# Two gate tiles join the seven-product quads, and the first two tiles of the attention mix are cut by heads and by high and low parts

## The chip, the cores and the metric

The kernel runs on one core of a Trainium2 chip. TensorE multiplies, VectorE (DVE), ScalarE (ACT) and GpSimd (POOL) work on the results, and SyncE (SP) and GpSimd start transfers between device memory and the on-chip buffer. The metric is the device time of one launch in microseconds (us). Three runs of the kernel before took 1771.04 to 1771.19 us, with a median of 1771.18.

## What is computed

One layer of a decoder over 1024 tokens of width 1024. The part that the change touches is the merge of three mixers:

```
z  = xn @ W_in            # q | k | v | conv B | conv C | conv h | pool u | 3 branch gates of 1024
gates  = sigmoid(z[gates] + b_gate)
merged = gates[A] * (y_attn @ w_attn_proj)      # the attention mix: y_attn is 1024 tokens x 8 heads of 128
       + gates[B] * (y_conv @ w_conv_proj)
       + gates[C] * (y_pool @ w_pool_proj)      # y_pool = (trailing means of u - u), times small matrices
x = x + rms_norm(merged @ w_out);  x = x + rms_norm(SwiGLU(rms_norm(x)))
```

## The kernel before

**Precision.** Every fp32 operand is held as a high part (`HH`) and a low part (`LL`), and a product is three passes (`PASSES`): high by high, high by low, low by high. A matmul is 128x128 weights against 512 tokens. A plain tile of 128 output columns over 1024 tokens is thus 2 halves x 8 blocks x 3 passes = 48 matmuls (`job`, or `half_job` for one half).

**Quads.** Most of `W_in` from the convolution's columns on is worked in pairs of tiles by seven products of 12 matmuls in place of eight (`x_quad` on each engine; the list is `XQ`, 16 quads long). The sums of inputs that this needs are held in `s_op1` to `s_op4`. A quad's seventh product, `x_third` (weights `B22`, operand `s_op4`), is put into the next quad, since it goes into a bank that the others must have left. The quads use two sets of three of the eight PSUM banks in turn. Each quadrant of a result is combined by DVE, put through the sigmoid by ACT in `stage`, and stored to device memory by POOL (the stores in its `x_quad` loop, semaphores `stage_stored`).

**The end of the quads.** The last two gate tiles (2048+768 to 2048+1023 of the gates) are plain tiles: the first half of one, then the last quad's `x_third`, then the other three halves. After them comes the attention mix: eight tiles of `w_attn_proj`, whose moving operand `ya` (high and low part of eight heads) lies where `s_op1` to `s_op4` lay. POOL's `load_ya` brings `ya` in four transfers of 2 MB, each when the products that read the `s_op` under it are done; the last of them, the low part of heads 4 to 7, waits for `x_third`. TensorE waits for all four before the mix.

**What follows on the other engines.** POOL stores the two plain gate tiles, loads gates (`load_gate`, three buffers, two of them over `stage` and one over the raw sums) and loads the pooling input `u` into `u_pad` (four transfers of 512 KB), which lies over `xn`. DVE goes through the mix tiles in a fixed order (the loop over `m`): it makes the low part of the next weight tile, works out the pooling difference `d_raw` from `u_pad` (`pool_d(m)`, for m below 4), and only then multiplies the mix tile `m` out of PSUM by its gate into `merged`. The four banks 0 to 3 go round: mix tile m+2 (or a small pooling product put between) may start when the tile before in its banks is taken out. The weight ring has two slots, so tile m+2's weights are split after tile m is done. SP loads weights in the order in which they are split (`load`). All order is written out by hand and held by semaphores.

Of the kernel before, what the change touches and what calls it, by code (L numbers as in the profile page):

```python
# [72 lines left out]
def build(nc, x, g_pre_mix, w_in, b_gate, lambda_q1, lambda_k1, lambda_q2, lambda_k2, subln_g,  # L73
# [21 lines left out]
    G_TAIL = 2 * TT + 8  # L95
    G_ATTN = G_TAIL + 4
    G_CONV = G_ATTN + 2 * KT + 2 * 4
# [5 lines left out]
    with ctx:  # L103
# [144 lines left out]
        def proj_bank(first, part):  # L248
# [74 lines left out]
                     ("B12", 0): (first_landed[6], 32), ("B12", 1): (first_landed[7], 48),  # L323
                     ("B22", 0): (first_landed[7], 48), ("B12", 2): (x_pair_landed[0], 160),
                     ("B22", 1): (x_pair_landed[0], 160), ("B22", 2): (x_pair_landed[1], 144)}
        d_landed = [sem(f"d_landed{i}") for i in range(6)]
# [6 lines left out]
        out_stored = x_first[1]  # L333
        x1_landed = tail_stored[0]


# [25 lines left out]
        for j in (0, 2):  # L362
            XQ += [("U", OFF_POOL + j * P, j * P), ("G", OFF_GATE + D + j * P, D + j * P)]
        XQ += [("G", OFF_GATE + D + j * P, D + j * P) for j in (4, 6, 8, 10, 12)]
        NQ = len(XQ)
        X_QUAD_BANKS = (BANKS[1], BANKS[0])

# [97 lines left out]
        def _(sp):  # L465
# [49 lines left out]
            sp.wait_ge(x_products, made(NQ - 1, "P1"))  # L515
            for j in range(6, 8):
                load(tile_of(w_in, OFF_GATE + 2 * D + P * j))
            for m in range(KT):
# [111 lines left out]
        def _(pool):  # L630
# [142 lines left out]
            def load_ya(part, half, products):  # L773


                pool.wait_ge(x_products, products)
                h = slice(4 * half, 4 * half + 4)
                pool.dma_start(ya[:, part, h, :].bitcast(F32),
                               y_dram[h].rearrange("h p (s t) -> p s h t", s=2)[:, part]).then_inc(y_landed, 16)

# [40 lines left out]
            load_gate(0)  # L821
            for j in range(2):
                for half in range(2):
                    gi = G_TAIL + 2 * j + half
                    pool.wait_ge(evacuated[gi % 4], gi // 4 + 1)
                pool.dma_start(gate_dram[2 * D + P * (6 + j):2 * D + P * (7 + j), :], stage[:, j, :])\
                    .then_inc(tail_stored[j], 16)
            pool.wait_ge(tail_stored[0], 16)
            load_gate(1)

            pool.wait_ge(groups_done, G_ATTN)
            for b in range(4):
                pool.wait_ge(stage_stored[b], 16 * quads_of("GU", NQ))
            for c in range(4):
                pool.dma_start(u_pad[:, c, 16:16 + S], u_dram[P * c:P * (c + 1), :]).then_inc(u_landed, 16)
            for buf in (u_pad[:, :, 0:16], sum_a[:, 0:16], sum_b[:, 0:16]):
                pool.memset(buf, 0.0).then_inc(pads_ready, 1)
            pool.wait_ge(tail_stored[1], 16)
            load_gate(2)
            for n in range(3, 18):  # L840
# [116 lines left out]
        def _(act):  # L957
# [336 lines left out]
            direct_part(NQ - 1)  # L1294
            for j in range(2):
                if j:
                    split_next()
                for b in (2 * j, 2 * j + 1):
                    act.wait_ge(stage_stored[b], 16 * quads_of("GU", NQ))
                sigmoid(lambda half: part_of(stage, j, half), bias_g[:, 2 * KT + 6 + j:2 * KT + 7 + j])  # L1300

# [7 lines left out]
            for m in range(KT):  # L1309
                split_next()  # L1310
                if m == 0:
                    split(w_pool[:, HH].rearrange("p g c -> p (g c)"), elems=512, free=(groups_done, g.at()))
                if m < 4:
                    act.wait_ge(d_ready, 2 * m + 2)
                    copy(yp[:, HH, m, :], d_raw[:, :]).then_inc(d_hi, 1)
                else:
                    split(yc[:, HH, m - 4, :], free=(d_lo, 4))
                g.next(2)
                if 2 <= m < 6:
                    pool_out(m - 2)  # L1320
# [225 lines left out]
        def _(dve):  # L1546
# [353 lines left out]

            for j in range(2):
                split_next()
                g.next(2)

# [38 lines left out]
            for m in range(KT):  # L1943
                split_next()
                if m == 0:
                    split(lambda s: w_pool[:, s].rearrange("p g c -> p (g c)"), elems=512)
                if m < 4:
                    pool_d(m)
                else:
                    split(lambda s: yc[:, s, m - 4, :])  # L1950
# [335 lines left out]
            for g in range(4, STEPS):  # L2286
# [15 lines left out]
                if g >= 5 * FC + 5 and g % 2 == 0 and (g - 5 * FC - 5) // 2 < 4:  # L2302
                    if g == 5 * FC + 5:
                        dve.wait_ge(g3_landed, 16)
                        dve.wait_ge(x1_landed, 16 * (TT + 1))
                    finish((g - 5 * FC - 5) // 2)
# [12 lines left out]
        def _(pe):  # L2319
# [263 lines left out]
            pe.wait_ge(xs_lo, 1)  # L2583
            for j in range(2):
                wait_evacuated(pe, g, j - 4)
            for q in range(NQ):
                x_quad(q)
            half_job(xn, 0)
            x_third(NQ - 1)
            half_job(xn, 1)  # L2590
            job(xn)

# [4 lines left out]

            pe.wait_ge(y_landed, 16 * 4)
            for m in range(KT):
                job(ya)  # L2600
                if m == 1 or m >= 5:

                    n.next()
# [181 lines left out]
```

## Time and profile before

| what | value |
|---|---|
| median of three runs | 1771.18 us |
| the profiled execution | 1771.71 us, its span 1769.8 us |
| TensorE busy | 1758.9 us, 99% of the span, 8497 matmuls |
| DVE, ACT, POOL busy | 65%, 42%, 14% |
| granted TensorE clock | 0.999 on average |
| DMA | 213.68 MB, 121 GB/s on average |

Times in the rows are microseconds from the first instruction of the span. A row of the timeline merges equal instructions that follow each other: its start, how long they took together, engine, line, operation, what is written from what is read, and the count. A bracket at the end gives the idle time of that engine before the row and who ended it. TensorE's ends are modelled, so the step from one row's start to the next is the better measure than the length that it gives. The line numbers are those of the helpers for most matmuls and for all splits.

### The profile page before, as it was taken

How to read it: one execution, taken by the hardware profiler on the slowest of the kernel's cores; microseconds unless marked ns; L12 is line 12 of the kernel's file. 1: busy time of each engine (PE TensorE's matmuls, PEld its weight loads, DVE VectorE, ACT ScalarE, POOL GpSimd, SP SyncE). 2: the span in 40 equal slices, each digit the busy share in tenths (PEclk: the TensorE clock that was granted, in tenths of full speed). 3: DMA queues.
4: the chain of work that ended last, by engine and by line, in shares of the span. 5: the costliest groups of instructions: out<-in, count | busy, mean ns of one | idle time of the engine just before them, and what ended most of it. 6: DMA issues, size and time to landing. Idle time of an engine off the chain costs nothing.

```text
span 1769.8 us, 25045 instructions
## 1 busy us (share of the span) xinstructions
PE 1758.9 (99%) x8497; PEld 1455.0 (82%) x8497; DVE 1151.7 (65%) x1863; ACT 739.1 (42%) x1486; POOL 250.7 (14%) x557
## 2 busy tenths in 40 slices
PE   9999999999999999999999999999999999999998
PEld 7887888888888888888888888888888888888886
DVE  5328989999885774443465655776665655567676
ACT  5316666666743323443231123343333333344553
POOL 3221222222120001111100102101010000000011
PEclk9999999999999999999999999999999999999999
DMA  7421222222142222326735712223232322673443
GB/s 242 144 84 49 72 73 71 72 71 71 51 145 87 88 65 99 128 101 230 251 108 168 247 60 95 96 95 126 106 107 102 117 89 94 232 280 98 147 142 125
DMA packets 138041, 213.68 MB, mean 121 GB/s; under 512 B 7569, under 2 KB 94097, under 8 KB 136930
## 3 DMA queue, kind: packets, MB, share of 16 engines
q1 hardware_dynamic: 109200, 108.54, 19.4%
q0 software_dynamic: 28752, 104.04, 16.2%
q8 instruction: 46, 0.75, 0.2%
q14 instruction: 41, 0.34, 0.1%
q10 hardware_dynamic: 2, 0.00, 0.0%
HBM read 150.17 MB, written 62.39 MB: 120 GB/s over the span
## 4 chain that ended last, share of the span: by engine, by line
PE 98%; DVE 1%; issue 0%; ACT 0%; DMA 0%; POOL 0%; DVEq 0%; POOLq 0%; ACTq 0%
PE ps L2340 26%; PE ps L2672 22%; PE ps L2540 17%; PE ps L2728 12%; PE ps L2424 11%; PE ps L2440 4%; PE ps L2348 3%; PE ps L2462 2%; PE ps L2464 1%; DMA x_tile<-in_x_dram 0%; DVE pt L1559 0%; DVE ring L1559 0%; DVE neg_max L1672 0%; DVE ps L1669 0%; ACT e_t L1084 0%
## 5 line engine op out<-in xcount | busy, mean ns | idle before, releaser
L2728 PE MATMUL ps<-d_op 128*128 128x512 f32 x924 | 210.3, 389 | 0.1
L2728 PEld LDWEIGHTS ps<-d_op 128*128 128x128 f32 x924 | 173.3, 188 | 36.9 <-DVE d_op L1559 0.5
L2672 PE MATMUL ps<-s_op,t_op_T 128*128 128x512 f32 x720 | 169.9, 389 | 0.0
L2424 PE MATMUL ps<-xn,ring 128*128 128x512 f32 x672 | 167.1, 398 | 0.0
L2672 PEld LDWEIGHTS ps<-s_op,t_op_T 128*128 128x128 f32 x720 | 135.2, 188 | 28.0
L2424 PEld LDWEIGHTS ps<-xn,ring 128*128 128x128 f32 x672 | 122.5, 188 | 24.8 <-issue 0.2
L2540 PE MATMUL ps<-s_op,x_op_T 128*128 128x512 f32 x576 | 135.9, 389 | 0.0
L2540 PEld LDWEIGHTS ps<-s_op,x_op_T 128*128 128x128 f32 x576 | 108.1, 188 | 22.4
L2672 PE MATMUL ps<-hn,t_op_B 128*128 128x512 f32 x480 | 115.1, 389 | 0.0
L2672 PEld LDWEIGHTS ps<-hn,t_op_B 128*128 128x128 f32 x480 | 90.1, 188 | 18.7
L1084 ACT ACTIVATE e_t<-ps,neg_max 128x256 f32<-128x256 f32 (+7 forms) x128 | 94.1, 740 | 16.5 <-DVE neg_max L1672 15.1
L1559 DVE TENSOR_TENSOR t_op_B<-pair,t_op_B 128x512 fp32r<-128x512 f32 x60 | 41.4, 689 | 90.8 <-ACT t_op_B L963 90.8
L963 ACT ACTIVATE d_op<-rf_pieces 128x512 fp32r<-128x512 f32 x87 | 53.8, 629 | 106.6 <-PE ps L2728 101.1
L1559 DVE TENSOR_TENSOR d_op<-rf_pieces,d_op 128x512 fp32r<-128x512 f32 x87 | 59.3, 691 | 59.9 <-ACT d_op L963 59.9
L1672 DVE TENSOR_REDUCE neg_max<-ps 128x1 f32<-128x256 f32 (+7 forms) x128 | 91.0, 752 | 2.2
L2540 PE MATMUL ps<-xn,x_op_B 128*128 128x512 f32 x384 | 92.1, 389 | 0.0
L2340 PE MATMUL ps<-w_v,xn 128*128 128x512 f32 x384 | 90.5, 395 | 0.0
L2340 PE MATMUL ps<-w_o,ring 128*128 128x512 f32 x384 | 89.0, 391 | 0.0
L2340 PE MATMUL ps<-ya,ring 128*128 128x512 f32 x384 | 87.8, 389 | 0.0
L2340 PEld LDWEIGHTS ps<-w_v,xn 128*128 128x128 f32 x384 | 72.4, 190 | 15.1 <-DVE xn L1559 0.3
L2540 PEld LDWEIGHTS ps<-xn,x_op_B 128*128 128x128 f32 x384 | 72.1, 188 | 14.9
L2340 PEld LDWEIGHTS ps<-ya,ring 128*128 128x128 f32 x384 | 72.1, 188 | 14.9
(270 smaller groups left out, 3374.7 us busy)
## 6 DMA issues: line engine op xcount, KB each, us to landing
pair<-in_w_gate_up_dram SPq DMA_DIRECT2D x20, 1024.0 KB, 5.2
rf_pieces<-s_scratch SPq DMA_DIRECT2D x74, 256.0 KB, 2.7
x_pair<-in_w_in_dram SPq DMA_DIRECT2D x16, 1024.0 KB, 6.2
raw<-in_w_in_dram SPq DMA_DIRECT2D x26, 512.0 KB, 4.0
s_scratch<-gated_ff POOLq DMA_DIRECT2D x40, 256.0 KB, 2.5
gate_in<-gate_scratch POOLq DMA_DIRECT2D x18, 512.0 KB, 3.8
v_scratch<-v_out POOLq DMA_DIRECT2D x32, 256.0 KB, 2.6
vh<-v_scratch POOLq DMA_DIRECT2D x16, 512.0 KB, 5.3
```

Of the source, the lines that this page charges most:

```text
L963: return act.activation(dst, src, ACT.Copy, **kw)
L1084: act.activation(e_t[:, i % 2, c, 0:w], ps[:, 2 * c:2 * c + 2, :].rearrange("p a b -> p (a b)")[:, 0:w], ACT.Exp, bias=neg_max[:, i % 2, c ...
L1559: return dve.tensor_tensor(dst, src, hi.bitcast(F32), ALU.subtract)
L1672: dve.tensor_reduce(neg_max[:, i % 2, c:c + 1], ps[:, 2 * c:2 * c + 2, :].rearrange("p a b -> p (a b)")[:, 0:P * (i + 1)], AX_X, ALU.max, ...
L2340: last = pe.matmul(ps[:, bank, :], lhs, rhs, start=i == 0, stop=i == len(pairs) - 1)
L2348: last = pe.transpose(ps[:, TB[b], P * k:P * (k + 1)], src[:, P * k:P * (k + 1)], ident[:, :])
L2424: last = pe.matmul(ps[:, proj_bank(first, half), :], proj_weights(which, par, a)[:, P * k:P * (k + 1)], xn[:, b, k, HALF * half:HALF * (ha ...
L2440: last = pe.matmul(ps[:, 2 * c + chunk, 0:w], qt[rows, par, a, P * i:P * (i + 1)], kt[rows, par, b, HALF * chunk:HALF * chunk + w], start= ...
L2462: pe.matmul(ps[:, U_BANK, 0:2 * HV], pt[:, i % 2, HH, k, :], vh[:, par, :, k, :], start=k == 0, stop=k == i, skip_group_check=True)
L2540: last = pe.matmul(ps[:, bank, :], x_op[name][:, a, k, :], block(b, k), start=opens and (k, a, b) == (0, HH, HH), stop=(k, a, b) == (3, LL ...
L2672: last = pe.matmul(ps[:, bank, :], t_op[name][:, a, k, :], block(b, k), start=opens and (k, a, b) == (0, HH, HH), stop=(k, a, b) == (3, LL ...
L2728: last = pe.matmul(ps[:, DOWN_BANKS[product][i], :], d_op[:, g % 4, a, P * i:P * (i + 1)], d_op[:, g % 4, 2 + b, :], start=opens and (a, b ...
```

## The change

The two plain gate tiles become a 17th quad in `XQ`. The set of banks that a quad starts with is turned round, so that the last quad again uses banks 4 to 6 and leaves banks 0 to 3 to the mix. The mix's tiles 0 and 1 are worked by `mix_part`: the passes that read the high part of `ya` (two of three) for heads 0 to 3 of tile 0, then the last quad's `x_third`, then the high passes of heads 4 to 7, then those of tile 1, and at the end the passes that read the low part, of tile 0 and then of tile 1. Each of the four transfers of `ya` has its own semaphore, and TensorE waits for each where it is first read. POOL no longer stores the plain tiles and no longer waits for their products; it waits until the last quad's quadrants are stored, loads gates 1 and 2, and then `u`.

```diff
-    G_ATTN = G_TAIL + 4
+    G_ATTN = G_TAIL
...
+        ya_landed = {(HH, 0): (y_landed, 16), (HH, 1): (tail_stored[1], 16), (LL, 0): (early_stored[0], 16 * 5),
+                     (LL, 1): (early_stored[1], 16 * 3)}
...
-        XQ += [("G", OFF_GATE + D + j * P, D + j * P) for j in (4, 6, 8, 10, 12)]
+        XQ += [("G", OFF_GATE + D + j * P, D + j * P) for j in (4, 6, 8, 10, 12, 14)]
         NQ = len(XQ)
-        X_QUAD_BANKS = (BANKS[1], BANKS[0])
+        X_QUAD_BANKS = BANKS
...
             sp.wait_ge(x_products, made(NQ - 1, "P1"))
-            for j in range(6, 8):
-                load(tile_of(w_in, OFF_GATE + 2 * D + P * j))
...
             pool.wait_ge(xt_lo, 7 * NQ)
             load_gate(0)
-            for j in range(2):
-                for half in range(2):
-                    gi = G_TAIL + 2 * j + half
-                    pool.wait_ge(evacuated[gi % 4], gi // 4 + 1)
-                pool.dma_start(gate_dram[2 * D + P * (6 + j):2 * D + P * (7 + j), :], stage[:, j, :])\
-                    .then_inc(tail_stored[j], 16)
-            pool.wait_ge(tail_stored[0], 16)
-            load_gate(1)
-
-            pool.wait_ge(groups_done, G_ATTN)
             for b in range(4):
                 pool.wait_ge(stage_stored[b], 16 * quads_of("GU", NQ))
+            for n in (1, 2):
+                load_gate(n)
             for c in range(4):
                 pool.dma_start(u_pad[:, c, 16:16 + S], u_dram[P * c:P * (c + 1), :]).then_inc(u_landed, 16)
...
-            pool.wait_ge(tail_stored[1], 16)
-            load_gate(2)
...
-            for j in range(2):
-                if j:
-                    split_next()
-                for b in (2 * j, 2 * j + 1):
-                    act.wait_ge(stage_stored[b], 16 * quads_of("GU", NQ))
-                sigmoid(lambda half: part_of(stage, j, half), bias_g[:, 2 * KT + 6 + j:2 * KT + 7 + j])
...
-            half_job(xn, 0)
-            x_third(NQ - 1)
-            half_job(xn, 1)
-            job(xn)
...
-            pe.wait_ge(y_landed, 16 * 4)
-            for m in range(KT):
+            def mix_part(m, part, heads, opens=False, closes=False):
+
+                for half in range(2):
+                    for k in heads:
+                        for a, b in PASSES:
+                            if b == part:
+                                last = pe.matmul(ps[:, g.slot(4, 2 * m + half), :], ring[:, r.slot(2, m), a, P * k:P * (k + 1)],
+                                                 ya[:, b, k, HALF * half:HALF * (half + 1)],
+                                                 start=opens and k == heads[0] and a == HH,
+                                                 stop=closes and k == heads[-1], skip_group_check=True)
+                    if closes:
+                        last.then_inc(groups_done, 1)
+
+
+            job_weights()
+            pe.wait_ge(*ya_landed[HH, 0])
+            mix_part(0, HH, range(4), opens=True)
+            x_third(NQ - 1)
+            pe.wait_ge(*ya_landed[HH, 1])
+            mix_part(0, HH, range(4, KT))
+            job_weights()
+            mix_part(1, HH, range(KT), opens=True)
+            for half in range(2):
+                pe.wait_ge(*ya_landed[LL, half])
+            for m in range(2):
+                mix_part(0, LL, range(KT), closes=True)
+                g.next(2)
+                r.next()
+            n.next()
+            for m in range(2, KT):
                 job(ya)
```

On TensorE, from the last quad's sixth product on, the program before reads as follows. `x_op` and `s_op` are a quad's operands, `xn,ring` the plain gate tiles, `ya,ring` the mix.

```order
L2540 MATMUL ps<-s_op_53,x_op_T_87 128x512 x11
L2340 MATMUL ps<-xn,ring 128x512 [waits evacuated0,w_lo]
L2340 MATMUL ps<-xn,ring 128x512 x23
L2540 MATMUL ps<-s_op_54,x_op_B_88 128x512 [waits x_combined,xs_lo,xt_lo]
L2540 MATMUL ps<-s_op_54,x_op_B_88 128x512 x11
L2340 MATMUL ps<-xn,ring 128x512 [waits evacuated1]
L2340 MATMUL ps<-xn,ring 128x512 x23
L2340 MATMUL ps<-xn,ring 128x512 [waits evacuated2,w_lo]
L2340 MATMUL ps<-xn,ring 128x512 x23
L2340 MATMUL ps<-xn,ring 128x512 [waits evacuated3]
L2340 MATMUL ps<-xn,ring 128x512 x23
L2340 MATMUL ps<-ya,ring 128x512 [waits evacuated0,w_lo,y_landed]
```

In the changed program the same place of the same engine reads:

```order
L2526 MATMUL ps<-s_op_53,x_op_T_87 128x512 x11
L2587 MATMUL ps<-ya,ring 128x512 [waits y_landed,w_lo]
L2587 MATMUL ps<-ya,ring 128x512 x15
L2526 MATMUL ps<-s_op_54,x_op_B_88 128x512 [waits x_combined,xs_lo,xt_lo]
L2526 MATMUL ps<-s_op_54,x_op_B_88 128x512 x11
L2587 MATMUL ps<-ya,ring 128x512 [waits tail_stored1]
L2587 MATMUL ps<-ya,ring 128x512 x15
L2587 MATMUL ps<-ya,ring 128x512 [waits w_lo]
L2587 MATMUL ps<-ya,ring 128x512 x31
L2587 MATMUL ps<-ya,ring 128x512 [waits early_stored1,early_stored0]
L2587 MATMUL ps<-ya,ring 128x512 x31
L2326 MATMUL ps<-ya,ring 128x512 [waits evacuated0,w_lo]
```

The 96 plain matmuls are gone from between the quads and the mix (84 of their work now stand in the quad ahead), the wait for the low half of `ya` stands behind 64 high matmuls of the mix and `x_third`, and the first wait for an emptied bank (`evacuated0`) is that of mix tile 2.

On POOL, behind the store of the last quad's quadrant (`gate_scratch<-stage` on `direct_act`), the program before reads as follows; `L812` is `load_gate`, `L826` the store of a plain gate tile, `L835` the load of `u`.

```order
L778 DMA ya<-y_scratch 128x4x1024 [waits x_products]
L807 DMA gate_scratch<-stage 128x512 [waits direct_act]
L812 DMA gate_in<-gate_scratch 128x1024 [waits xt_lo]
L826 DMA gate_scratch<-stage 128x1024 [waits evacuated1,evacuated0]
L826 DMA gate_scratch<-stage 128x1024 [waits evacuated3,evacuated2]
L812 DMA gate_in<-gate_scratch 128x1024 [waits tail_stored0]
L835 DMA u_pad<-u_scratch 128x1024 [waits stage_stored2,stage_stored1,stage_stored3,stage_stored0,groups_done]
L835 DMA u_pad<-u_scratch 128x1024 x3
```

In the changed program:

```order
L779 DMA ya<-y_scratch 128x4x1024 [waits x_products]
L809 DMA gate_scratch<-stage 128x512 [waits direct_act]
L814 DMA gate_in<-gate_scratch 128x1024 [waits xt_lo]
L814 DMA gate_in<-gate_scratch 128x1024 [waits stage_stored2,stage_stored3,stage_stored1,stage_stored0]
L814 DMA gate_in<-gate_scratch 128x1024
L829 DMA u_pad<-u_scratch 128x1024 x4
```

The two stores and the waits for plain tiles are gone; gates 1 and 2 and then `u` stand behind the landing of the last quadrant's store alone.

On DVE, between the last split of a mix weight ahead of the loop and the first time that a mix tile is taken out of PSUM, the changed program reads (`L1905` to `L1913` are `pool_d(0)`, `L1941` takes mix tile 0 out):

```order
L1546 TENSOR_TENSOR ring<-raw,ring 128x1024 [waits w_hi]
L1546 TENSOR_TENSOR w_pool<-raw,w_pool 128x512 [waits conv_stored2,conv_stored3,conv_stored1,w_hi,conv_stored0,over_ready]
L1905 TENSOR_TENSOR sum_a<-u_pad 128x1024 [waits pads_ready,u_landed]
L1910 TENSOR_TENSOR first_w<-sum_a,over_t 128x2 [waits dve_step]
L1911 SCALAR_TENSOR_TENSOR d_raw<-sum_a,u_pad 128x1022 [waits dve_step]
L1913 TENSOR_TENSOR d_raw<-first_w,u_pad 128x2
L1941 TENSOR_TENSOR merged<-gate_in,ps 128x512 [waits groups_done,gate_landed2]
L1941 TENSOR_TENSOR merged<-gate_in,ps 128x512 [waits groups_done]
L1546 TENSOR_TENSOR yp<-d_raw,yp 128x1024 [waits d_hi]
L1546 TENSOR_TENSOR ring<-raw,ring 128x1024 [waits w_hi]
```

This order is that of the program before; only the two splits of plain gate weights ahead of it have gone.

## Rows read from the trace of the kernel before

**Rows 1.** The profile page: span, TensorE's busy time, the granted clock in 40 slices
```profile
span 1769.8 us, 25045 instructions
PE 1758.9 (99%) x8497; PEld 1455.0 (82%) x8497; DVE 1151.7 (65%) x1863; ACT 739.1 (42%) x1486; POOL 250.7 (14%) x557
...
PEclk9999999999999999999999999999999999999999
```

**Rows 2.** Timeline of TensorE around the end of the quads
```profile
829.36 5.60 PE L2340 MATMUL ps<-xn,ring 128*128 128x512 f32 x24
834.80 2.88 PE L2540 MATMUL ps<-s_op,x_op_B 128*128 128x512 f32 x12
837.52 16.48 PE L2340 MATMUL ps<-xn,ring 128*128 128x512 f32 x72
853.84 32.80 PE L2340 MATMUL ps<-ya,ring 128*128 128x512 f32 x144
886.48 1.52 PE L2340 MATMUL ps<-yp,w_pool 128*128 128x512 f32 x6
```

**Rows 3.** Timeline of POOL, the transfers that it starts there
```profile
824.38 0.76 POOL L778 DMA_DIRECT2D ya<-y_scratch  x1 [3.66 <-PE ps L2540]
...
829.82 0.76 POOL L778 DMA_DIRECT2D ya<-y_scratch  x1 [3.66 <-PE ps L2540]
...
837.98 0.76 POOL L778 DMA_DIRECT2D ya<-y_scratch  x1 [6.14 <-PE ps L2540]
838.73 0.54 POOL L807 DMA_DIRECT2D gate_scratch<-stage  x1
...
855.78 0.53 POOL L812 DMA_DIRECT2D gate_in<-gate_scratch  x1
856.31 2.09 POOL L835 DMA_DIRECT2D u_pad<-u_scratch  x4
```

**Rows 4.** Line 778, the four loads of `ya`: issue to landing
```profile
DMA to landing us min/median/max: 9.3/10.9/11.6
```

**Rows 5.** Line 778 from 829 to 830.5 us, the load begun at 829.82
```profile
DMA to landing us min/median/max: 11.2/11.2/11.2
```

**Rows 6.** Line 807 from 836.5 to 840 us, the last quadrant's store
```profile
DMA to landing us min/median/max: 11.5/11.5/11.5
```

**Rows 7.** Line 835 from 855 to 860 us, the four loads of `u`
```profile
DMA to landing us min/median/max: 6.3/7.8/9.5
```

**Rows 8.** Stretches: busy time and count by engine, clock, DMA share, GB/s
```profile
840.00:845.00 5.00, 5.00 (x24) 4.13 (x22) 0.00 (x0) 2.20 (x3) 0.40 (x1) 1.00 1.06 386
845.00:850.00 5.00, 5.00 (x24) 4.14 (x23) 1.23 (x1) 0.01 (x1) 0.14 (x1) 1.00 1.02 408
860.00:865.00 5.00, 5.00 (x24) 4.14 (x23) 0.00 (x0) 0.00 (x0) 0.00 (x0) 1.00 1.01 389
```

**Rows 9.** Timeline of ACT and of SP, a row each
```profile
850.25 0.69 ACT L1066 ACTIVATE stage<-ps,bias_g 128x512 f32<-128x512 f32 x1 [5.24 <-DMA gate_scratch<-stage]
...
857.06 24.39 SPq L475 DMA_DIRECT2D raw<-in_w_attn_proj_dram  x4
```

**Rows 10.** Timeline of DVE from the landing of `u`
```profile
867.41 1.23 DVE L1920 TENSOR_TENSOR sum_a<-u_pad 128x1024 f32<-128x1024 f32 x1 [9.77 <-DMA u_pad<-u_scratch]
...
870.08 1.28 DVE L1955 TENSOR_TENSOR merged<-gate_in,ps 128x512 f32<-128x512 f32 x2
...
872.43 1.22 DVE L1559 TENSOR_TENSOR ring<-raw,ring 128x1024 fp32r<-128x1024 f32 x1
...
886.16 1.27 DVE L1955 TENSOR_TENSOR merged<-gate_in,ps 128x512 f32<-128x512 f32 x2
```

**Rows 11.** Timeline of TensorE at the start of the program
```profile
7.71 1.97 PE L2348 MATMUL ps<-ident,xs_tile 128*128 128x128 f32 x8 [0.42 <-DVE xs_tile L1590]
...
10.24 9.64 PE L2340 MATMUL ps<-w_v,xn 128*128 128x512 f32 x36
19.72 1.03 PE L2348 MATMUL ps<-ident,xs_tile 128*128 128x128 f32 x8
```

More of the change, by code:

```diff
@@ L323, in build @@
                      ("B12", 0): (first_landed[6], 32), ("B12", 1): (first_landed[7], 48),
-                     ("B22", 0): (first_landed[7], 48), ("B12", 2): (x_pair_landed[0], 160),
-                     ("B22", 1): (x_pair_landed[0], 160), ("B22", 2): (x_pair_landed[1], 144)}
+                     ("B22", 0): (first_landed[7], 48), ("B12", 2): (x_pair_landed[0], 176),
+                     ("B22", 1): (x_pair_landed[0], 176), ("B22", 2): (x_pair_landed[1], 144)}
         d_landed = [sem(f"d_landed{i}") for i in range(6)]
@@ L778, in load_ya @@
                 pool.dma_start(ya[:, part, h, :].bitcast(F32),
-                               y_dram[h].rearrange("h p (s t) -> p s h t", s=2)[:, part]).then_inc(y_landed, 16)
+                               y_dram[h].rearrange("h p (s t) -> p s h t", s=2)[:, part])\
+                    .then_inc(ya_landed[part, half][0], 16)
             for q, (kind, _, row0) in enumerate(XQ):
@@ L1309, in _ @@
             for m in range(KT):
-                split_next()
                 if m == 0:
-                    split(w_pool[:, HH].rearrange("p g c -> p (g c)"), elems=512, free=(groups_done, g.at()))
+                    split(w_pool[:, HH].rearrange("p g c -> p (g c)"), elems=512, free=(x_products, 7 * NQ))
+                else:
+                    split_next()
                 if m < 4:
@@ L1899, in _ @@
                 x_quad(q)
-            for j in range(2):
-                split_next()
-                g.next(2)
+            split_next()
             def gate_of(n, c=0):
@@ L1943, in _ @@
             for m in range(KT):
-                split_next()
                 if m == 0:
                     split(lambda s: w_pool[:, s].rearrange("p g c -> p (g c)"), elems=512)
+                else:
+                    split_next()
                 if m < 4:
@@ L2304, in _ @@
                         dve.wait_ge(g3_landed, 16)
-                        dve.wait_ge(x1_landed, 16 * (TT + 1))
+                        dve.wait_ge(x1_landed, 16 * TT)
                     finish((g - 5 * FC - 5) // 2)
@@ L2583, in _ @@
             pe.wait_ge(xs_lo, 1)
-            for j in range(2):
+            x_quad(0)
+            for j in range(4):
                 wait_evacuated(pe, g, j - 4)
-            for q in range(NQ):
+            for q in range(1, NQ):
                 x_quad(q)
-            half_job(xn, 0)
-            x_third(NQ - 1)
-            half_job(xn, 1)
-            job(xn)
             def pool_group(c):
@@ L2596, in pool_group @@
                     group((w_pool[:, a, c, :], yp[:, b, c, HALF * half:HALF * (half + 1)]) for a, b in PASSES)
-            pe.wait_ge(y_landed, 16 * 4)
-            for m in range(KT):
+            def mix_part(m, part, heads, opens=False, closes=False):
[25 more added lines that the diff above has]
+            for m in range(2, KT):
                 job(ya)
-                if m == 1 or m >= 5:
+                if m >= 5:
                     n.next()
```

## Prediction

> **What bounds the kernel now.** I read the page first: TensorE is busy for 1758.9 of 1769.8 us, and the clock row shows 9 in all forty slices [rows 1]. So only two things can move the time: the number of matmuls, and new waits of TensorE. The timeline of TensorE around the change shows the pace, 24 matmuls from 829.36 to 834.80, that is 0.2267 us each, and no idle time from the quads into the mix and up to the first small pooling product at 886.48 [rows 2]. Then I read, for everything that the new order lets TensorE reach earlier, who delivers it and when: POOL's transfers and their landings [rows 3 to 7], the load of the DMA engines [rows 8], and the chain on DVE that starts when `u` lands [rows 10]. The reader is to see that TensorE, although never late, is followed closely: mix tile 2 starts at 853.84 + 96 x 0.2267 = 875.60, and DVE finished that tile's weights at 872.43 + 1.22 = 873.65 [rows 2, 10]. The slack is 2.0 us.
>
> I call T the end of the last quad's sixth product. It is 829.36 before [rows 2]; after the change it comes one quad (84 x 0.2267 = 19.04 us) later, and what surrounds it in the quads is the same steady pattern, so I cost the 17th quad at its matmuls alone. The DVE and ACT work that it adds lies under them as in the sixteen others; if it did not, the quads ahead would show waits, and the timeline has none. The turned banks of the first quad wait for buffers that two plain tiles (21.8 us) have let go: nothing.
>
> **The matmuls.** The two plain tiles are 96 matmuls, the quad 84: 12 fewer, 2.72 us gained. The cut mix has the same matmuls: 16 + 12 (`x_third`) + 16 + 32 + 32, then tile 2. Without waits tile 2 starts at T + 108 x 0.2267 = T + 24.5. Before, it started at T + 46.2.
>
> **The wait for `ya`.** The high parts: the second of them was issued at T - 5.0 and took at least 9.3 us, so T + 4.3, wanted at T + 6.35: no wait [rows 3, 4]. The low parts are wanted at T + 76 x 0.2267 = T + 17.2. The first was issued at 829.82 and landed 11.2 later, T + 11.7 [rows 3, 5]. The second waits for `x_third`, which ends at T + 8.2 before and at T + 6.35 after; it took up to 11.6 us, landing at 849.6 = T + 20.2 [rows 3, 4]. Is it earlier by the same 1.8 us? The DMA engines were full, share 1.06 and 1.02 at 386 and 408 GB/s, from before it was issued until it was in [rows 8], and the load ahead of it on the same queue landed at 841.0, 3 us after it was issued. So I take T + 19.9, between T + 18.4 (the same latency) and T + 20.2 (the same landing). That is a wait of 2.7 us, 1.2 to 3.0. It is not added, since a longer one swallows it.
>
> **The load of `u`.** This is the term that decides. Before, POOL issued `u` at 856.31, T + 26.9, after a plain tile's store, and it landed at 867.4 = T + 38.0, where DVE had idled for it 9.77 us; TensorE was then busy with mix tiles 0 and 1 [rows 3, 7, 10]. After, `u` is wanted much earlier: tile 2 needs bank 0, DVE empties bank 0 only after `pool_d(0)`, and `pool_d(0)` waits for all of `u`. From the landing of `u`, DVE reached the mix tile after 2.67 us and had split tile 2's weights after 6.24 us (867.41 to 873.65), ACT's share included [rows 10]. So TensorE starts tile 2 at the landing plus 6.24, and without a wait `u` must land by T + 18.2.
>
> It can't. POOL may issue gates 1 and 2 and `u` only when the last quadrant's store has landed. That store stood right behind the last `ya` load, took 11.5 us, and ended at 850.2 = T + 20.9; ACT, which waited for it, went on at 850.25 [rows 3, 6, 9]. After the change it is issued some 1.2 us earlier into the same full queue. With the last `ya` load at T + 19.9 I take T + 20.5, between T + 19.1 (issue at T + 7.6 with the same latency) and T + 20.9. From there to the landing of `u`: before, from the issue of a gate at 855.78 to 867.4 were 11.6 us, with about 2 MB of other traffic around (another store of 512 KB, SP's weights from 857.06 [rows 9]). After, six transfers of 512 KB, 3.15 MB, at 389 GB/s [rows 8] need at least 8.1 us; the most is the 11.6 of before plus one more gate, 1.3 us, so 12.9. I take 10.6, in the middle, as there is one gate more and less of the rest. `u` lands at T + 31.1; bounds T + 27.2 and T + 33.8.
>
> TensorE starts tile 2 at T + 37.3 in place of T + 24.5: 12.9 us of idle time, in two pieces (about 2.7 before the low products, about 10 before tile 2).
>
> **What follows the stall.** TensorE now runs right behind DVE. Tile 2 and the pooling product end 10.88 + 1.36 later, at landing + 18.5; tile 3 needs the bank that DVE empties by 886.16 + 0.69, landing + 19.4 [rows 10]: 0.96 us more. TensorE also restarts after 10 us of rest. The clock is full in every slice [rows 1] and TensorE rests only ahead of its first instructions, so no row shows a fall; the nearest is the start of the program, where eight transposes took 1.97 us against 1.03 later, the pace of 1.2 against 2.4 GHz, and the next 36 matmuls took 9.48 us where the full pace gives 8.16, a loss of 1.32 [rows 11]. Zero is the low end for the clock and twice that, 2.6, the high one. The two hide each other, as a slower tile 2 waits less for DVE: I take 1.3 for both, 0.96 to 2.6. The Trainium skill, "TensorE: Matmul & The Clock Gate", section "Why this matters for your kernels", speaks against this change: it says that idle gaps between bursts put the engine back to half clock. By it the 1.3 is due; without it the sum has 0.96.
>
> **Sum.** -2.72 + 12.9 + 1.3 = +11.4 us. Bounds: -2.72 + (27.2 + 6.24 - 24.5) + 0.96 = +7.2, and -2.72 + (33.8 + 6.24 - 24.5) + 2.6 = +15.4. The profiled execution would go from a span of 1769.8 to 1781.2 and from 1771.7 to 1783.1; it lies 0.5 us above the median of the runs, so the median goes to 1782.6.
>
> **Rivals.**
> Faster, 6%: no stall at all. The place is the wait of DVE for `u`; it decides at a landing of T + 18.2. If the last quadrant's small store landed as soon as it would on an empty queue and `u` was let through beside the `ya` loads, only the 12 matmuls would count: -2.7 us, 1768.5. For it speaks only that the issue is early (T + 7.6). Against it: the 2 MB of `ya` behind which it stands, 11.5 us of latency, and 3.15 MB still to come at 389 GB/s. This is also the case in which the change does what its matmul count says.
>
> No difference, 3%: only the wait for the low part of `ya` counts, T + 20.2 against T + 17.2, 3.0 us lost and 2.7 gained: +0.2, 1771.4. It needs `u` in by about T + 21, which the same bytes exclude unless the DMA engines gave far more than 408 GB/s.
>
> Slower still, 15%: SP's weight loads get in the way of `u`. SP may issue a further tile as soon as `w_pool` is split, and up to two tiles (1.05 MB) can fall between the store and `u`; at 389 GB/s that is 2.7 us on my landing: +14.1, 1785.3. The four of 857.06 were started in that very place before [rows 9], so part of it is in the 11.6 already. The Trainium skill, "DMA: Bandwidth & Descriptors", section "Queues, rings and completion order", says that each DMA engine takes turns between the queues that have work for it; by that, SP's two tiles would hold the POOL queue back by their own bytes at most, as in this rival. The full share in [rows 8] fits it.
>
> The forecast, 76%: 1782.6, its own range 1779.5 to 1785.
>
> **Chances.** This kernel can tell 0.2% (3.5 us) from no change. Faster by more than that would be below 1767.6, which takes the first rival and luck besides, 2%; within it, 1767.7 to 1774.7, lie the two small rivals and a landing of `u` some 8 us earlier than I think, 8%; slower 90%. The range for 8 in 10 takes the bounds of the sum nearly whole: 1778.4 to 1786.6, by the median.
>
> **What would show it.** Right: TensorE idle for 9 to 14 us in one stretch after the 32 low products of the mix, put down to DVE; a smaller wait of 1 to 3 us ahead of those products, put down to a DMA; DVE waiting for `u_pad` until about 31 us after the sixth product of the last quad; the last quadrant's store taking 10 us or more to land; 12 matmuls fewer; the clock row below 9 in the slice of the stall, or at least matmuls of 0.43 us behind it. Wrong: the first load of `u` issued before T + 15, tile 2 starting at T + 24.5, or a wait inside the 17 quads. If `u` lands as said but tile 2 starts more than 8 us later, the chain of 6.24 us was the step that failed; if the idle time is right and the sum is not, it is the clock or a later wait.

## The result, and the profile after

The changed kernel took 1785.28 us (median of 6 runs, 1783.80 to 1786.67) against 1771.23 us before (6 runs, 1771.04 to 1772.36): ratio 1.0078, 95% interval 1.0065 to 1.0091. It is 14.05 us slower, where 11.4 us were forecast. That is inside the range for 8 in 10 (1778.4 to 1786.6), 0.3 us above the forecast's own range (1779.5 to 1785), and on the number of the rival called "slower still" (1785.3). The profiled execution has a span of 1783.8 us against 1769.8 [rows 1]: 14.0 us.

The page of the changed kernel has 12 matmuls fewer, and for the first time a slice in which TensorE is busy for 6 tenths only, and a slice of its clock below 9:

```profile
span 1783.8 us, 25048 instructions
PE 1759.3 (99%) x8485; PEld 1453.8 (82%) x8485; DVE 1158.6 (65%) x1875; ACT 742.4 (42%) x1494; POOL 251.6 (14%) x559
...
PE   9999999999999999999699999999999999999998
...
PEclk9999999999999999999899999999999999999999
```

Busy time hides the gain: it went up by 0.4 us although 12 matmuls are gone, as some of the others ran slowly. The list of TensorE's waits names the place (engine, line, released by: us in total, times, longest):

```profile
PE ps L2326 <- DVE ring L1546: 11.0, 1, 11.0
PE ps L2587 <- DMA ya<-y_scratch: 2.6, 1, 2.6
```

In TensorE's timeline T, the end of the last quad's sixth product, is at 848.96. The rows answer to [rows 2]:

```profile
848.96 3.79 PE L2587 MATMUL ps<-ya,ring 128*128 128x512 f32 x16
852.58 2.88 PE L2526 MATMUL ps<-s_op,x_op_B 128*128 128x512 f32 x12
855.30 11.04 PE L2587 MATMUL ps<-ya,ring 128*128 128x512 f32 x48
868.97 7.52 PE L2587 MATMUL ps<-ya,ring 128*128 128x512 f32 x32 [2.63 <-DMA ya<-y_scratch]
887.44 12.87 PE L2326 MATMUL ps<-ya,ring 128*128 128x512 f32 x48 [10.95 <-DVE ring L1546]
900.15 1.52 PE L2326 MATMUL ps<-yp,w_pool 128*128 128x512 f32 x6
```

Tile 2 starts at T + 38.5 in place of T + 24.5, and takes 900.15 - 887.44 = 12.71 us where full pace gives 10.88. The second bracket says "DVE ring": the event that came last was the split of tile 2's weights. What held DVE stands one step further back. POOL's transfers, answering to [rows 3]:

```profile
855.76 0.76 POOL L779 DMA_DIRECT2D ya<-y_scratch  x1 [4.32 <-PE ps L2526]
856.51 0.54 POOL L809 DMA_DIRECT2D gate_scratch<-stage  x1
857.04 0.54 POOL L814 DMA_DIRECT2D gate_in<-gate_scratch  x1
870.19 1.06 POOL L814 DMA_DIRECT2D gate_in<-gate_scratch  x2 [12.61 <-DMA gate_scratch<-stage]
871.24 2.09 POOL L829 DMA_DIRECT2D u_pad<-u_scratch  x4
```

POOL stood for 12.61 us on the landing of one 256 KB store, which took 13.1 us (line 809, answering to [rows 6]):

```profile
DMA to landing us min/median/max: 13.1/13.1/13.1
```

DVE, answering to [rows 10], waited 22 us for `u`, then took out tile 0, then split tile 2's weights:

```profile
881.15 1.23 DVE L1905 TENSOR_TENSOR sum_a<-u_pad 128x1024 f32<-128x1024 f32 x1 [21.98 <-DMA u_pad<-u_scratch]
...
883.82 1.28 DVE L1941 TENSOR_TENSOR merged<-gate_in,ps 128x512 f32<-128x512 f32 x2
...
886.17 1.22 DVE L1546 TENSOR_TENSOR ring<-raw,ring 128x1024 fp32r<-128x1024 f32 x1
```

Landing at T + 32.2, and 6.29 us from there to TensorE's tile 2. The clock, by stretches (the column ahead of the DMA share), answers to [rows 8]:

```profile
874.00:880.00 6.00, 2.49 (x11) 1.72 (x10) 0.00 (x0) 0.00 (x0) 0.00 (x0) 1.00 0.96 370
880.00:882.00 2.00, 0.00 (x0) 0.00 (x0) 0.85 (x1) 0.00 (x0) 0.00 (x0) 0.70 0.08 31
882.00:884.00 2.00, 0.00 (x0) 0.00 (x0) 1.93 (x5) 0.06 (x1) 0.00 (x0) 0.50 0.00 0
...
888.00:890.00 2.00, 2.00 (x6) 1.57 (x5) 1.91 (x3) 0.00 (x0) 0.00 (x0) 0.50 0.70 208
890.00:892.00 2.00, 2.00 (x8) 1.52 (x8) 1.99 (x4) 0.66 (x1) 0.00 (x0) 0.74 0.32 91
892.00:894.00 2.00, 2.00 (x10) 1.66 (x9) 2.00 (x3) 1.35 (x2) 0.53 (x1) 1.00 0.03 9
```

It fell to half, 1.2 GHz, while TensorE rested, and was back at 2.4 GHz before tile 2 ended.

The 14.0 us of the span thus are: 12 matmuls, -2.72; tile 2 later by 14.0 against its T; its slow pace, +1.83; T itself 0.56 later than one quad accounts for; and +0.33 behind the mix's first pooling product. For the last two TensorE's list has no wait. T, whose place nothing in the later variants touches, lay between 848.0 and 849.4 in the twelve profiles with 17 quads, where one quad more than before gives 848.4. The 0.33 us arise by the time that the first 36 matmuls on `hn` are done, as they do in z1 and z3; their cause stays open.

### The profile page after: what moved, and what is told of

Its sections match the earlier page's. It is cut to its first block and busy times, and to the rows that moved or that the text cites. A ratio compares the mean times of both kernels' runs of the same rounds, so it can differ in the third digit from the quotient of the medians.

```text
span 1783.8 us, 25048 instructions
## 1 busy us (share of the span) xinstructions
PE 1759.3 (99%) x8485; PEld 1453.8 (82%) x8485; DVE 1158.6 (65%) x1875; ACT 742.4 (42%) x1494; POOL 251.6 (14%) x559
## 5 line engine op out<-in xcount | busy, mean ns | idle before, releaser
L2526 PE MATMUL ps<-s_op,x_op_T 128*128 128x512 f32 x612 | 144.4, 389 | 0.0
L2526 PEld LDWEIGHTS ps<-s_op,x_op_T 128*128 128x128 f32 x612 | 114.9, 188 | 23.9
L2526 PE MATMUL ps<-xn,x_op_B 128*128 128x512 f32 x408 | 97.8, 389 | 0.0
L2526 PEld LDWEIGHTS ps<-xn,x_op_B 128*128 128x128 f32 x408 | 76.6, 188 | 15.9
L1546 DVE TENSOR_TENSOR x_op_B<-x_pair,x_op_B 128x512 fp32r<-128x512 f32 x51 | 35.0, 690 | 81.9 <-ACT x_op_B L955 81.9
L2326 PEld LDWEIGHTS ps<-w_o,ring 128*128 128x128 f32 x384 | 71.6, 188 | 15.0 <-issue 0.4
```

What stands on the lines that cost most here:

```text
L1546: return dve.tensor_tensor(dst, src, hi.bitcast(F32), ALU.subtract)
L2326: last = pe.matmul(ps[:, bank, :], lhs, rhs, start=i == 0, stop=i == len(pairs) - 1)
L2526: last = pe.matmul(ps[:, bank, :], x_op[name][:, a, k, :], block(b, k), start=opens and (k, a, b) == (0, HH, HH), stop=(k, a, b) == (3, LL ...
```

## The experiments

"Before" is the kernel before, run beside the variant on the same chip. The variants ran on more than one chip, so they are compared by their differences from it.

| kernel | median us | before | difference | 95% interval of the ratio |
|---|---|---|---|---|
| changed kernel | 1785.28 | 1771.23 | +14.1 | 1.0065 to 1.0091 |
| x1_order | 1780.21 | 1772.01 | +8.2 | 1.0031 to 1.0064 |
| x2_u_early | 1781.25 | 1772.01 | +9.2 | 1.0036 to 1.0070 |
| x4_warm | 1785.04 | 1772.01 | +13.0 | 1.0059 to 1.0093 |
| x5_whole | 1787.93 | 1772.01 | +15.9 | 1.0074 to 1.0108 |
| x3_low | 1784.50 | 1771.79 | +12.7 | 1.0058 to 1.0089 |
| y1_order2 | 1772.73 | 1771.79 | +0.9 | 0.9996 to 1.0015 |
| y2_order_u | 1773.75 | 1771.79 | +2.0 | 1.0001 to 1.0019 |
| y3_all | 1773.39 | 1771.79 | +1.6 | 1.0005 to 1.0023 |
| z2 | 1772.77 | 1771.44 | +1.3 | 0.9998 to 1.0017 |
| z1 | 1770.83 | 1771.44 | -0.6 | 0.9988 to 1.0006 |
| z3 | 1769.97 | 1771.44 | -1.5 | 0.9983 to 1.0001 |

**x1_order: is it DVE's place behind `u`?** On DVE (ACT follows):

```diff
-            for m in range(KT):   # split, pool_d(m), take mix tile m out, low part of d, pool_out(m - 2)
+            split(lambda s: w_pool[:, s].rearrange("p g c -> p (g c)"), elems=512)
+            for m in range(2):
+                mix_out(m)
+                split_next()
+            difference_of(0)
+            for m in range(1, 4):
+                mix_out(m + 1)
+                difference_of(m)
+                pool_out(m - 1)
+                if m < 3:
+                    split_next()
+            split(lambda s: yc[:, s, 0, :])
+            for m in range(5, KT):   # split_next, split yc[m - 4], mix_out(m), at 5 also pool_out(3)
```

> DVE takes mix tiles 0 and 1 out of PSUM and splits the weights of tiles 2 and 3 before it waits for u; ACT's splits follow the same order. Theory (the stall is DVE's place in the queue behind u): the wait of 10.95 us ahead of tile 2 goes, and with it the low clock (1.8 us); the 2.6 us wait for the low part of ya stays, about 1772.5 us. Rival A (the transfers themselves hold TensorE, since the DMA engines are full): tile 2 still starts some 38 us after the last quad's sixth product, above 1782. Rival B (DVE has too much work there): the wait is only spread over the next tiles, 1778 or more.

Tile 2 followed the low products without a wait (875.42 = T + 26.7), and its 48 matmuls took 11.05 us, near the full pace of 10.88, though `u` landed as late as in the changed kernel (T + 32.5). The cause is shown: not the transfer as such, but that DVE waits for it ahead of taking tile 0 out. The size was missed, 8.2 us above the kernel before in place of 0.5, and the number fell where rival B had put it (1778 or more), since 5.0 us came back ahead of mix tile 6, at 924.9. DVE's and ACT's rows of x1_order there:

```profile
927.92 1.23 DVE L1555 TENSOR_TENSOR yc<-raw,yc 128x1024 fp32r<-128x1024 f32 x1 [3.52 <-ACT yc L955]
929.06 1.28 DVE L1942 TENSOR_TENSOR merged<-gate_in,ps 128x512 f32<-128x512 f32 x2
```
```profile
926.83 1.06 ACT L955 ACTIVATE yc<-raw 128x1024 fp32r<-128x1024 f32 x1 [3.91 <-DMA raw<-conv_scratch]
```

In my order the split of the second convolution tile stood ahead of taking out mix tile 5, for which TensorE waited. Its load was issued at 923.29, right behind DVE's split of the first one, and ACT could begin at 926.83.

**y1_order2: was it that split?**

```diff
             split(lambda s: yc[:, s, 0, :])
-            for m in range(5, KT):
+            split_next()
+            mix_out(5)
+            pool_out(3)
+            split(lambda s: yc[:, s, 1, :])
+            for m in range(6, KT):
```

> The order of x1_order with one more turn: mix tile 5 is taken out of PSUM, and the last pooling product, before the second convolution tile is split, on DVE and ACT. Theory: the 5.0 us wait of x1_order came from that split, which waits for its load (ACT idle 3.91 us for it) and stood ahead of the taking out; it goes, and of the changed kernel's stalls only the wait for ya is left: 1780.2 - 5 = 1775. Rival (DVE has more work there than time, 12 us of it having been moved against TensorE): the 5 us come back in another place, 1779 to 1780.

It was, and more: 7.3 us less against the kernel before than x1_order, 1772.73 us where 1775 was expected. The rest of 5.0 us had also cost the clock. TensorE of x1_order and its stretch (the clock is the column ahead of the DMA share):

```profile
929.89 24.56 PE L2346 MATMUL ps<-ya,ring 128*128 128x512 f32 x96 [5.00 <-DVE merged L1942]
954.29 43.68 PE L2346 MATMUL ps<-yc,ring 128*128 128x512 f32 x192
```
```profile
932.00:934.00 2.00, 2.00 (x6) 1.52 (x6) 1.41 (x2) 1.06 (x1) 0.00 (x0) 0.50 0.73 238
```

The 96 matmuls behind the wait took 24.4 us where full pace gives 21.8: 2.6 us more, and this is what my expectation of 1775 left out. In the profile of y1_order2 what is left of the stalls is 2.12 us for `ya`, 1.7 us of slow pace behind it, and 0.26 us ahead of mix tile 6. This execution took 1773.65 us, 0.9 above the median; the last section comes back to the slow pace.

```profile
867.69 9.15 PE L2611 MATMUL ps<-ya,ring 128*128 128x512 f32 x32 [2.12 <-DMA ya<-y_scratch]
876.68 11.04 PE L2350 MATMUL ps<-ya,ring 128*128 128x512 f32 x48
```

**x2_u_early: how much is POOL's wait for the store, how much the bytes?**

```diff
+            last_u = max(q for q, (kind, _, _) in enumerate(XQ) if kind == "U")
+            for b in range(4):
+                pool.wait_ge(stage_stored[b], 16 * quads_of("GU", last_u + 1))
+            # the four loads of u and the memsets stand here
             for b in range(4):
                 pool.wait_ge(stage_stored[b], 16 * quads_of("GU", NQ))
             for n in (1, 2):
                 load_gate(n)
```

> POOL issues the loads of u right after gate 0, without waiting for the last quadrant's store (it waits only for the stores of u itself); gates 1 and 2 follow behind. Theory: of the 32 us to the landing of u, the wait for the store and the gap of the queue count, the bytes stay; u lands about 28 us after the sixth product in place of 32.2, so about 4 us less, 1781. Rival (the bytes alone set it): 1784 to 1786. Rival (u now pushes the last ya load back): the wait for ya grows beyond 2.6 us and the gain is smaller.

As the theory had it: 4.8 us less against the kernel before than the changed kernel. DVE and TensorE of x2_u_early (T is 848.98):

```profile
876.44 1.23 DVE L1908 TENSOR_TENSOR sum_a<-u_pad 128x1024 f32<-128x1024 f32 x1 [17.20 <-DMA u_pad<-u_scratch]
```
```profile
882.73 13.34 PE L2329 MATMUL ps<-ya,ring 128*128 128x512 f32 x48 [6.93 <-DVE ring L1549]
```

`u` was issued 13.6 us earlier (857.61 against 871.24), but landed only 4.7 earlier, at T + 27.5, where T + 18.2 was wanted. The edit takes away two things at once, the wait for the store and the two gates ahead of `u`, and no run tells them apart. An estimate from the rows: between 868 and 876 the DMA engines of the changed kernel stood idle for about 1.8 us (share 0.89, 0.30, 1.01 and 0.89 in stretches of 2 us), where those of x2_u_early had a share of 1.04 or 1.05; two gates of 512 KB at the 389 GB/s of [rows 8] are 2.7 us; together 4.5. The other 9.3 us are the transfers of `ya`, gate 0, SP's weights and `u` themselves, which keep the DMA engines full. The load of `ya` was not pushed back (wait 1.89).

**x4_warm: is tile 2's slow pace the clock?**

```diff
             n.next()
+            spare(5, 76)   # 76 transposes of the identity into bank 5
             for m in range(2, KT):
                 job(ya)
```

> 76 transposes of the identity (about 9.8 us) into a free bank on TensorE ahead of mix tile 2, inside the stall of 10.95 us. Theory (tile 2 took 12.7 us for 10.9 because the clock was at 1.2 GHz after the rest): tile 2 takes 10.9, the time falls by 1.8 to about 1783.5. Rival (tile 2 is slow for what it reads or waits for): nothing changes, 1785.3; if the filler reaches beyond the stall, more.

```profile
867.63 9.15 PE L2587 MATMUL ps<-ya,ring 128*128 128x512 f32 x32 [2.02 <-DMA ya<-y_scratch]
876.63 8.46 PE L2367 MATMUL ps<-ident 128*128 128x128 f32 x76
886.86 11.22 PE L2326 MATMUL ps<-ya,ring 128*128 128x512 f32 x48 [1.78 <-DVE ring L1546]
897.92 1.52 PE L2326 MATMUL ps<-yp,w_pool 128*128 128x512 f32 x6
900.16 11.17 PE L2326 MATMUL ps<-ya,ring 128*128 128x512 f32 x48 [0.72 <-DVE merged L1941]
```

Tile 2 started at the same place, T + 38.6, and took 11.06 us in place of 12.71: with TensorE kept at work, the pace was nearly full (10.88) and the granted clock 1.00. But the time fell by about 1 us, not 1.8, since the faster tile 2 met the next limit, 0.72 us of waiting for DVE to empty tile 3's bank. This is the term that the prediction had said the slow clock would hide (0.96), and that my expectation forgot. In the medians the two kernels can't be told apart, as their intervals overlap; the rows carry the verdict.

**x5_whole: what is taking the mix apart worth?**

```diff
-            job_weights() ... mix_part(1, HH, range(KT), opens=True) ... mix_part(0, LL, range(KT), closes=True) ...
+            x_third(NQ - 1)
+            for part in (HH, LL):
+                for half in range(2):
+                    pe.wait_ge(*ya_landed[part, half])
+            for m in range(KT):
                 job(ya)
```

> The 17th quad stays, the mix is not taken apart: x_third, then the wait for all of ya, then eight whole tiles. Theory: ya is in 19.9 us after the sixth product, two whole tiles take 21.8, so tile 2 starts at 41.7 in place of 38.5, about 3 us slower than the changed kernel, 1788.5, with the stall now put down to the ya transfer; taking the mix apart would be worth 3 us at most, since u holds its gain. Rival (without u in the way of it, the cut of the mix is worth all of its 76 matmuls, 17 us): 1798 or more.

```profile
867.75 34.76 PE L2326 MATMUL ps<-ya,ring 128*128 128x512 f32 x144 [15.58 <-DMA ya<-y_scratch]
```

TensorE waits 15.6 us for `ya`, and the kernel is only 1.9 us slower against the kernel before than the changed one (2.7 us by the plain medians). The cut hides 13 of these 15.6 us, and nearly all of that was lost again to `u`. The rival, 1798 or more, is excluded.

**x3_low: does the wait for `ya` count in the changed kernel?**

```diff
-            for half in range(2):
-                pe.wait_ge(*ya_landed[LL, half])
-            for m in range(2):
-                mix_part(0, LL, range(KT), closes=True)
+            pe.wait_ge(*ya_landed[LL, 0])
+            for m in range(2):
+                mix_part(m, LL, range(4))
+            pe.wait_ge(*ya_landed[LL, 1])
+            for m in range(2):
+                mix_part(0, LL, range(4, KT), closes=True)
                 g.next(2)
```

> The changed kernel with only the low passes reordered by heads, nothing else. Theory: the ya wait of 2.6 us goes or shrinks, but tile 2 still starts when DVE has u, so the wait ahead of it grows by the same: 1785, no change. Rival (the two waits add up): 1782.6.

```profile
854.56 18.29 PE L2587 MATMUL ps<-ya,ring 128*128 128x512 f32 x80
885.84 12.90 PE L2326 MATMUL ps<-ya,ring 128*128 128x512 f32 x48 [12.99 <-DVE ring L1546]
```

The 80 matmuls run through, so the `ya` wait is gone; the wait ahead of tile 2 grew from 10.95 to 12.99, and T to tile 2 is 37.6 us against 38.5. Against the kernel before it is 1.3 us less than the changed kernel (0.8 us by the plain medians), with intervals that overlap, and not 2.6; tile 2 started 0.9 us earlier because `u` landed 0.85 us earlier here (T + 31.3). The waits don't add.

**y2_order_u and y3_all: the two together, and with the low passes by heads.** The edits are those of y1_order2 and x2_u_early, in y3_all also that of x3_low.

> y1_order2 and the early loads of u (x2_u_early) together. Theory: with the mix taken out first, u has until the first pooling product; early or late makes under 1 us of difference to TensorE there, but DVE starts its 12 us of pooling differences 5 us sooner and what is left of waits behind it goes: 1772 to 1775. Rival (the two gains add up, 5 and 4 us): 1771 or less.

> y2_order_u, and the low passes of both mix tiles are done for heads 0 to 3 first (16 matmuls, 3.6 us) and only then wait for the second half of the low part. Theory: the wait for ya (1.9 to 2.6 us) is covered; tile 0 closes 1.8 us later, which leaves some 0.5 us of wait for tile 2's weights: 2 to 2.5 us less than y2_order_u, about 1770, 2 us below the kernel before, near its matmul count. Rival (tile 0's later closing costs what the wait gave): the same as y2_order_u.

y2_order_u came in inside its range (1773.75 us), but no better than y1_order2: +2.0 against +0.9 us. y3_all missed, with 1773.39 us where 1770 was expected: as its rival said, it is the same as y2_order_u. TensorE and then DVE of y3_all:

```profile
873.49 11.21 PE L2353 MATMUL ps<-ya,ring 128*128 128x512 f32 x48 [0.66 <-DVE ring L1560]
887.07 1.65 PE L2353 MATMUL ps<-yp,w_pool 128*128 128x512 f32 x6 [2.37 <-DVE yp L1560]
```
```profile
877.69 1.28 DVE L1947 TENSOR_TENSOR merged<-gate_in,ps 128x512 f32<-128x512 f32 x2 [4.25 <-DMA gate_in<-gate_scratch]
```

The `ya` wait is gone, but DVE now stands 4.25 us at mix tile 1 for gate 1, which x2_u_early's order has put behind `u`, and `pool_d(0)` queues behind it; in y2_order_u the same wait is 3.39 us. The same fault once more, with another transfer.

**z1, z2, z3: the order by landings.** z1 puts `pool_d(0)` ahead of mix tile 1; z2 is y1_order2 with the low passes by heads and `u` late; z3 is z1 with tile 0 closed 0.9 us earlier.

```diff
+            mix_out(0)
+            split_next()
+            pool_d(0)
+            mix_out(1)      # z1 and z3, then the low part of d and split_next()
```
```diff
             mix_part(0, LL, range(4))
+            mix_part(1, LL, range(4), halves=(0,))
             pe.wait_ge(*ya_landed[LL, 1])
             mix_part(0, LL, range(4, KT), closes=True)
+            mix_part(1, LL, range(4), halves=(1,))      # z3
             mix_part(1, LL, range(4, KT), closes=True)
```

> y3_all with DVE's first pooling difference ahead of mix tile 1 (which waits for gate 1), since u is in by then and gate 1 is not; early u and the low passes by heads stay. Theory: the wait of 2.37 us for the first pooling product in y3_all was gate 1's landing passed on by DVE's order; it goes, and 0.7 + 0.3 us of waits are left against 2.7 us of matmuls saved: about 1770, 1.5 to 2 below the kernel before. Rival (the DMA engines are full and each order only moves the wait): 1772 to 1774 again.

> y1_order2 (u late) with the low passes by heads, to tell the early u apart. Theory: the ya wait of 2.1 us and the slow restart behind it go, 0.7 us of wait for tile 2's weights and some 1.5 us for the first pooling product (u lands 32 us after the sixth product) come in: 1770.5 to 1771.5. Rival (a late u costs the whole of what the low passes give): 1772.7, as y1_order2.

> z1, and tile 0 closes 0.9 us earlier: the low passes of tile 1's second half for heads 0 to 3 stand behind tile 0's last ones. Theory: the wait of 0.7 us for tile 2's weights goes unless the last ya load lands later than 19.95 us after the sixth product: 0 to 0.7 us less than z1. Rival: no difference, since the last ya load then is waited for by as much.

z1 took 1770.83 us, outside its rival's 1772 to 1774, but only 0.6 us less than the kernel before, where 1.5 to 2 were expected; its interval includes no change. The wait of 2.37 us is gone, and 0.66 is left ahead of tile 2. z2 missed: its 1772.77 us are the rival's number. It has 0.66 us ahead of tile 2 and waits 1.85 us for the first pooling product, both near what was expected, but in the medians nothing is gained over y1_order2. In the profiled spans it is 0.9 us shorter (1770.8 against 1771.7), where the execution of y1_order2 was one of its slower ones. Between the medians of z2 and z1 lie 1.9 us, which the early `u` and the order that suits it are worth together: early `u` alone (y3_all against z2) gave nothing, and z1's order with a late `u` was not run. z3 is 0.9 us below z1, a little more than its theory allowed. z3 has no wait left there:

```profile
854.37 18.30 PE L2618 MATMUL ps<-ya,ring 128*128 128x512 f32 x80
872.51 11.07 PE L2357 MATMUL ps<-ya,ring 128*128 128x512 f32 x48
883.42 1.52 PE L2357 MATMUL ps<-yp,w_pool 128*128 128x512 f32 x6
```

Tile 2 starts at T + 24.5 (T is 848.03), as the count of matmuls says. z3 took 1769.97 us (11 runs, 1769.31 to 1770.86) against 1771.44 (26 runs): 1.5 us less, with an interval of 0.9983 to 1.0001, which just includes no change: a gain is likely and not proven. Its profiled span is 1.9 us shorter than before. At the first pooling product it is 3.1 us ahead (2.72 us of matmuls, and a T that is 0.4 earlier than costed); 0.26 us go to a wait ahead of tile 6, and some 0.9 in small steps behind it, without a wait of note.

## Why the prediction was right

**The step that decides, `u`, held.** The landing was put at T + 31.1 and was T + 32.2: POOL had the store and went on at T + 21.2 against T + 20.5, and from there to `u` 11.0 us against 10.6. The chain on DVE was 6.29 us against 6.24. Tile 2 was late by 14.0 us against 12.9. x1_order shows that DVE's order carries the lateness to TensorE, x2_u_early shows its two parts. A tile that was ready to be taken out waited for data that it doesn't use. Every sign that the prediction listed for being right came in, and none of those for being wrong.

**The matmuls held exactly**: 12 fewer, and no wait inside the 17 quads. Of their 2.72 us z3 gets 1.5 in the medians and 1.9 in the profiled span.

**The wait for `ya` held** in place and size: T + 20.0 against the T + 19.9 taken, 2.63 us against 2.7. Its load was issued at T + 6.8, 1.8 us earlier than before, and landed 0.3 us earlier (849.6 - 829.36 = 20.2 before, 855.76 + 13.1 - 848.96 = 19.9 after). The size was a little lucky: in the ten other profiles with the cut mix the same load landed at T + 19.0 to T + 19.7, so that the earlier issue gave 0.3 to 1.2 of its 1.8 us. x3_low shows that this wait was covered, as stated.

**The clock was there and under-sized**: 1.83 us against 1.3 for it and the wait of tile 3 together. That the two hide each other is shown by x4_warm. The price had come from the start of the program. The loss after this rest was larger, and that the loss of 1.32 us at the start was the clock was inferred: the profile before gives the granted clock as 1.00 from 10 to 12 us, where only 6 matmuls ran in place of 9.

**The miss of 2.7 us** in the medians, 14.1 against 11.4, is nearly made up in the profiled execution of `u` (+1.1), the clock (+0.5), and the 0.9 us for which no wait stands in the list. A small slip changes nothing: the prediction says that the last quadrant's store is issued some 1.2 us earlier, and reckons with T + 7.6, which is 1.8 earlier and what was measured (T + 7.55).

**The rivals.** The measured time is the number of "slower still", 1785.3, but not by its mechanism: it had two tiles of SP's weights between the store and `u`, 2.7 us on the landing, and `u` was 1.1 us late. In the trace SP issued a single tile between the store's issue and the landing of `u`, and the next at 887.41, behind it:

```profile
859.20 0.37 SPq L478 DMA_DIRECT2D raw<-in_w_attn_proj_dram  x1
```

It landed 13.1 us later, at 872.3, so it ran beside the store and only at its end beside the gates and `u`. No run held SP's loads back, so what they add to the 13.1 us of the store stays open; its landing, T + 21.2 against T + 20.5, makes 0.7 of the 1.1 us. That the median meets this rival's number is chance. The case without a stall was ruled out by the bytes, as x2_u_early's T + 27.5 confirms even with the wait for the store gone, and with it the case in which only the wait for `ya` counts.

## What to carry to other kernels

When work is taken away in front of a busy engine, everything behind it is wanted earlier: list each delivery with its landing before, and the time at which it is now wanted, and look above all at transfers that wait for another transfer's landing on a full queue. An in-order engine that empties PSUM must not stand behind a wait for data that this emptying doesn't use; sort its work by when inputs land, anew after each change of the transfers' order. A wait that has been hidden is worth little until the next one is gone too: the cut of the mix hid 13 us of waiting for `ya` and gave 2 to 3.

## What the runs showed of the hardware

A short rest can cost the clock or not. After rests of 2.02 and 2.12 us (x4_warm and y1_order2) the granted clock fell to 1.2 GHz only when TensorE was at work again, and 32 matmuls took 9.00 and 8.99 us, where the same 32 took 7.34 in x1_order; after 2.63 us in the changed kernel, 1.92 in x1_order, 1.89 in x2_u_early and 1.71 in y2_order_u the clock stayed at 2.4 GHz and they took 7.3 to 7.4. x4_warm's stretches:

```profile
868.00:870.00 2.00, 2.00 (x8) 1.57 (x7) 0.00 (x0) 0.00 (x0) 1.11 (x3) 0.74 0.58 184
870.00:872.00 2.00, 2.00 (x6) 1.58 (x5) 0.00 (x0) 0.00 (x0) 2.00 (x4) 0.50 0.89 252
```

What decides between them I can't tell from these runs. In these two traces a wait of 2 us cost 3.7 in TensorE's time. It need not come in every execution of a kernel: of y1_order2's ten runs the four with a mean granted clock of 0.998 took 1773.34 to 1773.86 us, the profiled one among them, and the six with 0.999 took 1771.55 to 1772.95. The size fits, as an estimate: 1.7 us lost at half pace is 0.001 of 1771 us. For the runs without a profile, that it was this restart is not shown. z1 and z3, whose profiles have no rest of more than 0.7 us there, have 0.999 in all 22 runs.
